# Three norms between GEMM stages by token halves, under neighbouring tiles in half order; value blocks ahead of the projections; squares added on GpSimd

## The reference

```
def rms_norm(x, g):
    xf = x.astype(jnp.float32)
    y = xf * lax.rsqrt(jnp.mean(xf * xf, axis=-1, keepdims=True) + EPS)
    return (y * g.astype(jnp.float32)).astype(x.dtype)
...
        h = modulate(rms_norm(x, g_ffn1[l]), sh1, sc1)
        x = x + HALF_STEP * gt1 * swiglu(h, w_gu1[l], w_down1[l])
        h = modulate(rms_norm(x, g_mix[l]), sh2, sc2)
        x = x + gt2 * hybrid_mixer(h, w_in[l], gate_bias[l], g_q[l], g_k[l], g_mh[l], w_out[l])
        h = modulate(rms_norm(x, g_ffn2[l]), sh3, sc3)
        x = x + HALF_STEP * gt3 * swiglu(h, w_gu2[l], w_down2[l])
        x = rms_norm(x, g_final[l])
```

## Time and profile before

| | us |
|---|---|
| time, median of 3 runs | 3765.18 (3762.93 to 3768.85) |
| the profiled execution's own time | 3765.66 |
| its span | 3763.9 |
| TensorE busy | 3433.6 (91%) |
| VectorE busy | 1844.4 (49%) |
| ScalarE busy | 1248.7 (33%) |
| GpSimd busy | 216.6 (6%) |

### The profile page before, as it was taken

The page is one execution under the profiler, slowest core; times in us unless marked ns, Lnnn a source line. Parts: engine busy times, 40 slices in busy tenths (PEclk is TensorE's granted clock), DMA queues, the critical chain, the costliest instruction groups (busy, mean ns, idle before and its releaser), DMA issues.

```text
span 3763.9 us, 38813 instructions
## 1 busy us (share of the span) xinstructions
PE 3433.6 (91%) x16290; PEld 2754.4 (73%) x16290; DVE 1844.4 (49%) x2135; ACT 1248.7 (33%) x1626; POOL 216.6 (6%) x299
## 2 busy tenths in 40 slices
PE   5999999988897689989999999789889978997996
PEld 3888888866885578868888888458678846776885
DVE  6333333366535679453333333651289556226974
ACT  4111111145231168331111112532168355214753
POOL 0000000000100022000000000010011000101210
PEclk8999999999997699999999999989899989998998
DMA  4222221212742268222212221132342202315221
GB/s 193 99 71 76 93 76 67 79 68 90 178 153 84 54 95 95 69 79 73 90 62 84 84 90 45 35 107 86 109 57 40 76 11 86 114 68 102 45 62 45
DMA packets 156269, 309.73 MB, mean 82 GB/s; under 512 B 55256, under 2 KB 103164, under 8 KB 145088
## 3 DMA queue, kind: packets, MB, share of 16 engines
q1 hardware_dynamic: 95936, 215.52, 17.6%
q0 software_dynamic: 60160, 91.74, 11.2%
HBM read 255.04 MB, written 52.18 MB: 82 GB/s over the span
## 4 chain that ended last, share of the span: by engine, by line
PE 79%; DVE 11%; ACT 6%; issue 2%; DMA 2%; SPq 0%; ACTq 0%; DVEq 0%; POOL 0%
PE psum L612 58%; PE psum L881 5%; PE psum L895 4%; PE psum L871 4%; PE psum L640 2%; PE psum L975 1%; ACT attn_num L1335 1%; DVE h_lo L1532 1%; PE psum L965 1%; PE psum L711 1%; DVE w_lo L1482 1%; ACT attn_th L1326 1%; DMA fo_alt<-in_alternating 1%; PE psum L805 1%; DVE p_u L1619 1%
## 5 line engine op out<-in xcount | busy, mean ns | idle before, releaser
L612 PE MATMUL psum<-h_hi,w_hi 128*128 128x512 f32 x2112 | 833.5, 395 | 45.2 <-DVE h_lo L1532 26.8
L612 PE MATMUL psum<-h_lo,w_hi 128*128 128x512 f32 x2112 | 824.8, 391 | 0.0
L612 PE MATMUL psum<-h_hi,w_lo 128*128 128x512 f32 x2112 | 824.7, 390 | 0.0
L612 PEld LDWEIGHTS psum<-h_hi,w_hi 128*128 128x128 f32 x2112 | 398.3, 189 | 143.5 <-issue 46.3
L612 PEld LDWEIGHTS psum<-h_lo,w_hi 128*128 128x128 f32 x2112 | 398.7, 189 | 83.1 <-issue 2.7
L612 PEld LDWEIGHTS psum<-h_hi,w_lo 128*128 128x128 f32 x2112 | 398.2, 189 | 83.6
L1088 ACT ACTIVATE w_hi<-w_raw 128x2048 fp32r<-128x2048 f32 (+2 forms) x135 | 226.2, 1676 | 538.6 <-PE psum L612 454.8
L1482 DVE TENSOR_TENSOR w_lo<-w_raw,w_hi 128x2048 fp32r<-128x2048 f32 (+2 forms) x135 | 269.4, 1995 | 253.2 <-ACT w_hi L1088 252.5
L1581 DVE TENSOR_TENSOR gate<-gate,psum 128x1024 f32<-128x1024 f32 x44 | 53.7, 1221 | 608.1 <-PE psum L612 608.1
L612 PE MATMUL psum<-a_hi,w_hi 128*128 128x512 f32 x704 | 274.1, 389 | 3.4 <-DVE a_lo L1583 3.4
L612 PE MATMUL psum<-a_lo,w_hi 128*128 128x512 f32 x704 | 273.9, 389 | 0.0
(11 more groups left out here) (356 smaller groups left out, 5111.3 us busy)
## 6 DMA issues: line engine op xcount, KB each, us to landing
w_raw<-in_w_ada SPq DMA_DIRECT2D x52, 1024.0 KB, 4.9
w_raw<-in_w_gu SPq DMA_DIRECT2D x44, 1024.0 KB, 5.3
w_raw<-in_w_in SPq DMA_DIRECT2D x34, 1024.0 KB, 4.9
w_raw<-in_w_down SPq DMA_DIRECT2D x24, 512.0 KB, 3.6
w_raw<-in_w_out SPq DMA_DIRECT2D x12, 1024.0 KB, 6.3
w_raw<-in_w_down SPq DMA_DIRECT2D x16, 640.0 KB, 4.8
qk_hi_scratch<-p_out_hi POOLq DMA_DIRECT2D x18, 512.0 KB, 2.9
qk_lo_scratch<-p_out_lo POOLq DMA_DIRECT2D x18, 512.0 KB, 3.8
```

The lines of the kernel that those rows point to most:

```text
L612: mm = e.matmul(p.half[h], a[:, k * width + m * P:k * width + (m + 1) * P], b(k)[:, h * HALF:(h + 1) * HALF], start=(ends[0] and k == orde ...
```

## The change

It concerns FFN 1, the mixer's projection, the end of the mixer and FFN 2.

- **Half order.** The last down group of an FFN and `out_proj`'s tiles 4 to 7 are done for all tiles on half 0 and then for all tiles on half 1, each tile half in a bank of its own (`take_bank`). The last group has two blocks of 4 x 512 columns in place of four of 4 x 256. `x` is updated by halves; half 0's statistics product comes after the first tile of half 1, and its norm (`guess_half`, `shifted`, `modulated` as generators, stepped between the updates) runs beside the rest of half 1. Half 1's statistics product and norm run in the next stage.
- **Openings.** FFN stages begin with `opening`: the four tiles of gate/up blocks 0 and 1 on half 0, then on half 1; the statistics' pair is the fourth tile's place (`over`). `proj1` begins with the value blocks 4 and 5, half 0 of both and then half 1 of both. In the plan no `ada` block follows gate/up 0 and two follow gate/up 1.
- **GpSimd** adds the squares (`add_squares`) for the tiles in half order, in place of VectorE.
- In `proj1` the gate block follows the k blocks, and the last two ropes run on under blocks 12 and 6; the fence `proj1b` and the row work start behind block 6, not 12. `proj1` stages through two buffers in place of three. `sq` becomes one tensor of 1024 columns, activations `h` are kept by halves, and tiles are placed anew in SBUF so that a norm's tiles and the stage before it don't overlap.

```
-PROJ_ORDER = (0, 1, 2, 3, 4, 5, 12, 6, 7, 8, 9, 10, 11)
+PROJ_ORDER = (4, 5, 0, 1, 2, 3, 12, 6, 7, 8, 9, 10, 11)
+LAST_GROUP = len(FF_GROUPS) - 1
...
+V_ORDER = ((4, 0), (5, 0), (4, 1), (5, 1))
+P1_ORDER = [("v", 2 * (b - 4) + half) for b, half in V_ORDER] + [("qk", i) for i in range(8)]
...
     def plan_ffn(n):
         for kind, i in ffn_order():
             if kind == "gu":
                 plan.append(("w", ins[f"w_gu{n}"][i], (BLK,), ("gu", n, i)))
-                plan_ada(1)
+                plan_ada({0: 0, 1: 2}.get(i, 1))
             else:
-                for c in range(4):
-                    plan.append(("w", columns(ins[f"w_down{n}"][FF_START[i]:FF_START[i + 1]], c), (FF_GROUPS[i], 256),
-                                 ("down", n, i, c)))
+                for c in range(4 if i < LAST_GROUP else 2):
+                    plan.append(("w", columns(ins[f"w_down{n}"][FF_START[i]:FF_START[i + 1]], c, 256 if i < LAST_GROUP else HALF),
...
-        if b >= 4:
+        if b == 3 or b >= 6:
...
+        def opening(stage, stat, tiles_, hi, lo, between):
+
+
+            pp = []
+            for h in range(2):
+                for j, (n_, whi, wlo, key, emptied) in enumerate(tiles_):
+                    if h == 0:
+                        pp.append(ps.take(e, key, *emptied) if j < 3 else ps.over(ps.give(("stat", stat)), key, *emptied))
+                    mm = tile(pp[j].half[h], j % 2, h, KT, whi, wlo, hi, lo,
+                              ready_at=(lambda k, h: h_lo.at(stage, k, h)) if j == 0 else None)
+                    if h == 0 and j == 0:
+                        between()
+                    if h == 1:
+                        mm.then_inc(*tile_done.mark(*key))
+                        if j % 2:
+                            tile_done.value[("block", n_)] = tile_done.count
...
+        def stat_half(stage, h, acc, *event):
+
+            e.wait_ge(*summed_g.at(*event))
+            mm = e.matmul(ps.of[("stat", stage)].half[h], mean1024, acc[:, h * HALF:(h + 1) * HALF], start=True, stop=True)
+            mm.then_inc(*sum_done.mark(stage, h))
...
+            places = [block(("gu", n, i)) for i in range(2)]
+            tiles_ = [(*places[i], (what, n, i), (emptied, n, i))
+                      for i in range(2) for what, emptied in (("gate", gate_silu), ("up", gated))]
+            opening(stage, stat, tiles_, hi, lo, (lambda: None) if n == 1 else
+                    (lambda: stat_half("after mix", 1, t.mix1.acc, "mix", KT - 1, 1)))
...
+                places = [block(("down", n, i, c)) for c in range(2)]
+                ps.take(e, ("stat", after), norm, "var", after, 1)
+                ps.keep(("stat", after))
+                for h in range(2):
+                    for dd in range(KT):
+                        n_, whi, wlo = places[dd // 4]
+                        bank = ps.take_bank(e, ("down", n, i, dd, h), x_new, stage, "half", dd, h)
+                        mm = tile(bank, dd % 4, h, nf, whi, wlo, a_hi_, a_lo_, width=HALF,
+                                  ready_at=(lambda k, h: a_lo.at(n, f0 + k)) if h == 0 and dd == 0 else None)
+                        mm.then_inc(*tile_done.mark("down", n, i, dd, h))
+                        if h == 1 and dd == 0:
+                            stat_half(after, 0, f.g, stage, KT - 1, 0)
...
+            places = {b: block(("in1", b)) for b in (4, 5)}
+            for j, (b, half) in enumerate(V_ORDER):
+                key, (n_, whi, wlo) = ("in1", 2 * b + half), places[b]
+                p = ps.take(e, key, out_lo, key) if j < 3 else ps.over(ps.give(("stat", "after ffn1")), key, out_lo, key)
+                gemm_rows(p, key, half, whi, wlo, m.h, ready_at=(lambda k, h: h_lo.at("mix", k, h)) if b == 4 else None,
+                          between=(lambda: stat_half("after ffn1", 1, t.ffn[1].g, "ffn1", KT - 1, 1)) if j == 0 else None,
+                          block_end=n_ if half else None)
...
+            places = [block(tag + (c,)) for c in (2, 3)]
+            after = f"after {stage}"
+            ps.take(e, ("stat", after), norm, "var", after, 1)
+            ps.keep(("stat", after))
+            for h in range(2):
+                for dd in range(4, KT):
+                    n_, whi, wlo = places[dd // 2 - 2]
+                    bank = ps.take_bank(e, ("out", name, dd, h), x_new, stage, "half", dd, h)
+                    mm = tile(bank, dd % 2, h, KT, whi, wlo, hi, lo, order=order)
+                    mm.then_inc(*tile_done.mark("out", name, dd, h))
+                    if h == 1 and dd == 4:
+                        stat_half(after, 0, m.acc, stage, KT - 1, 0)
...
+            blocks.get(("down", n, LAST_GROUP, 0))
+            e.wait_ge(*a_lo.at(n, FF_TILES - 1))
+            place, m = Counter(), t.proj1
+            front = shifted("mix", m.norm, m.h, 3, 0) if n == 1 else iter(())
+            for h in range(2):
+                for dd in range(KT):
+                    square_half(stage, dd, h, f.g, place)
+                    if h == 1 and n == 1:
+                        if dd == 0:
+                            guess_half("after ffn1", m.norm, 0)
+                        if dd == 3:
+                            blocks.get(("down", n, LAST_GROUP, 1))
+                        if 3 <= dd < 7:
+                            steps(front, 2)
...
+            blocks.get(("down", n, LAST_GROUP, 0))
+            m = t.proj1
+            front = modulated("mix", "after ffn1", m.norm, m.h, "g_mix", 3, 4, 0) if n == 1 else iter(())
+            for h in range(2):
+                for dd in range(KT):
+                    c, key = slice(h * HALF, (h + 1) * HALF), ("down", n, LAST_GROUP, dd, h)
+                    e.wait_ge(*tile_done.at(*key))
+                    e.wait_ge(*x_new.at(stage, LAST_GROUP - 1, dd))
+                    e.scalar_tensor_tensor(out=t.x[:, dd, c], in0=ps.of[key], scalar=cols[:, 8 + dd:9 + dd],
+                                           in1=t.x[:, dd, c], op0=ALU.mult, op1=ALU.add).then_inc(
+                        *x_new.mark(stage, "half", dd, h))
+                    if h == 1 and n == 1:
+                        steps(front, {1: 1, 3: 2, 4: 2, 5: 2, 6: 2, 7: 2}.get(dd, 0))
+                        if dd == 4:
+                            blocks.get(("down", n, LAST_GROUP, 1))
...
+        front = modulated("ffn2", "after mix", f.norm, f.h, "g_ffn2", 6, 7, 0)
+        for h in range(2):
+            for dd in range(4, KT):
+                c, key = slice(h * HALF, (h + 1) * HALF), ("out", "mix1", dd, h)
+                e.wait_ge(*tile_done.at(*key))
+                e.scalar_tensor_tensor(out=t.x[:, dd, c], in0=ps.of[key], scalar=mod_cols(0, 5)[:, dd:dd + 1],
+                                       in1=t.x[:, dd, c], op0=ALU.mult, op1=ALU.add).then_inc(*x_new.mark("mix", "half", dd, h))
+                if h == 1:
+                    steps(front, {4: 0, 5: 4, 6: 5, 7: 3}[dd])
+                    if dd == 5:
+                        blocks.get(("out1", 3))
...
+        def add_squares(stage, items, acc):
+
+            place = Counter()
+            for dd, h in items:
+                c = slice(h * HALF, (h + 1) * HALF)
+                e.wait_ge(*squared.at(stage, dd, h))
+                if dd == 0:
+                    continue
+                j = place.next()
+                if dd == 4 and stage == "mix":
+                    e.wait_ge(*summed.at(stage, 3, h))
+                elif dd == 1:
+                    e.wait_ge(*squared.at(stage, 0, h))
+                else:
+                    e.wait_ge(*summed_g.now())
+                e.tensor_tensor(acc[:, c], acc[:, c], sqh[j % 2], ALU.add).then_inc(*summed_g.mark(stage, dd, h))
+                summed_g.value[(stage, "place", j)] = summed_g.count
```

More of the change, by code:

```diff
@@ L195, in step, with steps @@
             pending.remove(g)
+def steps(generator, n=99):
+    for _ in range(n):
+        next(generator, None)
 class Counter:
@@ L336, in memory @@
         with ExitStack() as sc:
-            f.h = split(f"h{n}", [P, KT, S], sc)
-            f.norm = modulated_tiles(f"nf{n}")
+            back = halves(f"h{n}b", sc)
+            with ExitStack() as over:
+                if n == 1:
+                    gap("norm", 32 * 1024, over)
+                f.norm = modulated_tiles(f"nf{n}", over)
             f.ah = rings(f"a{n}_hi", A_SLOTS, [P, S], F32R, sc)
@@ L341, in memory @@
             f.g = sb(f"gate{n}", [P, S], F32, sc)
+            f.h = list(zip(halves(f"h{n}a", sc), back))
     def rope_tiles(m, name, scope):
@@ L353, in memory @@
     with ExitStack() as hs:
-        m.h = split("hm", [P, KT, S], hs)
-        m.norm = modulated_tiles("nm")
+        front = halves("hma", hs)
         with ExitStack() as sc:
@@ L366, in memory @@
             m.QB = sb("ml_QB", [P, S], F32, sc)
+        with ExitStack() as sc:
+            gap("a_hi", 16 * 1024, sc)
+            m.norm = Box()
+            m.norm.t = rings("nm_t", 4, [P, HALF], F32, sc)
+            gap("a_lo", 16 * 1024, sc)
```

(25 more changed lines are left out.)

396 lines of the change are left out of this document (221 added, 175 removed).

## The result

The changed kernel takes 3826.22 us (median of 4 runs, 3824.84 to 3827.53) against 3767.01 us for the kernel before on the same chip; the ratio is 1.016, 95% interval 1.0148 to 1.0173. The direction was forecast, the size was not: +59 where +24 stood, and outside the range of 3775 to 3803. The profiled execution has a span of 3823.6 us. The page's first row (busy us, share of the span, instructions of each engine) shows TensorE busy 12.8 us longer than before, and in the rest of the 59.7 us by which the span grew, 47 us, it stands.

A forecast was written before the change was run, and what follows sets the result against it. The prediction took TensorE's GEMM as the bound, with 38 us at two norm borders all the edit could give. Terms (a) to (i) summed to +24.4 us, giving 3790 us, range 3775 to 3803.

The forecast's parts named there:

- (a): FFN 1's start: the first product waits for block 1's split instead of a bank, +1.6 us.
- (b): Third gate/up block of each opening: its raw buffer is held by an ada block, stalls of 4.9 and 5.4 us.
- (c): Last down group of both FFNs: TensorE waits for the second block's split, stall 6.8 less 1.7, +5.1 us each.
- (d): out_proj: the fourth block's split, until now hidden by tiles 4 and 5, makes TensorE wait, +6.8 us.
- (g): Norm before FFN 2: stall of 11.2 us, 15.2 us outside GEMM against 19.5, so -4.3 us.
- (i): Behind FFN 2: shorter half updates and squares, GpSimd's longer add, statistics product and wait put inside, +0.7 us.
- (h): Lower TensorE clock after waits: 2.0 us behind each of five new stalls in (b), (c) and (d), +10.0 us.
- (f): proj1: the 5.08 us wait at L640 goes, -5.1 and -1.9 us of clock; the rope turns' waits stay.
- (e): Norm before the mixer: TensorE stands 10.4 us, 14.8 us outside GEMM with clock against 18.7, so -3.9 us.
- rival 3: GpSimd and VectorE slow each other in the norms: upper bound +11 us, so 3801; chance 0.08.
- Rivals 1 and 2: 1: second block's split comes in time, 3752, chance 0.08; 2: only the third block is in time, 3775, chance 0.09.
- rival 1: Second block's split comes in time, so waits of (b), (c), (d) don't show: -13 us, 3752; chance 0.08.

The follow-up runs named there:

- late wait: Changed kernel, but TensorE waits for each list's second weight block only ahead of its first product with it: 3774.29 us, ratio 1.0011.
- four edits: Changed kernel with second-block wait delayed, block behind FFN 2's last group prepared, gate tile's bank emptied first, ada blocks reordered: 3729.79 us, ratio 0.9901.

## Why the size was wrong

**What held.** (a) +1.6, measured +1.4. (b) Stalls of 4.9 (its pieces give 15.7 less 10.9, so 4.8) and 5.4, measured 4.0 and 3.8: the sum of six pieces was 1 to 1.5 us too long. (c) 6.8, measured 6.64 and 6.44; the rows cited for it give 750.7 less 744.1, so 6.6. (d) 6.8, measured 6.73. (g) 11.2, measured 11.01. (i) within the forecast's 4.7 for its stretch, measured 4.6. The late wait shows the cause of six of the stalls in one run: (a), (c) twice, (d), (e) and (g). By these terms alone the forecast of a slower kernel was right for its reason.

**(h), the clock,** was a little small. The granted clock of the changed kernel in windows behind three of the stalls (window, its length, PE busy with products, granted clock, DMA share, GB/s):

```profile
757.52:763.00 5.48, 5.48 (x13) 0.52 0.58 193
763.00:769.00 6.00, 6.00 (x28) 1.00 0.00 1
112.65:118.00 5.35, 5.35 (x13) 0.53 0.60 196
1700.10:1705.00 4.90, 4.90 (x14) 0.65 0.61 214
```

Behind the stall of 6.64 us (first row) thirteen products take 5.48 us at 0.52, half of full speed, where 24 fit at 0.2267 us each: 2.5 us lost, where I took 2.0. After that it is 1.00. Behind the stall of 4.02 us 2.4 us are lost, nearly as much. Behind that of 3.79 us (last row) it is 1.7 us, because the low clock comes only with the sixth product:

```profile
1701.14 0.39 PE L660 MATMUL psum<-h2a_lo,w_hi 128*128 128x512 f32 x1
1701.36 0.55 PE L660 MATMUL psum<-h2a_hi,w_lo 128*128 128x512 f32 x1
1701.71 0.63 PE L660 MATMUL psum<-h2a_hi,w_hi 128*128 128x512 f32 x1
```

Over the five stalls of the term that makes about 11.6 us instead of 10.0. The Trainium skill (TensorE: Matmul & The Clock Gate, HAM oscillation) says that bursts parted by waits start at the lower clock each time. This trace agrees behind the stalls of 4.02 and 6.64 us, and not behind that of 3.79 us, whose burst began at full rate.

**The step that failed first** stands in no term of the sum. It is the sentence "The rest of the kernel is GEMM that the edit does not shorten", with the description's claim that the edit leaves the second layer as it is but for names: the start of the second layer was put at nothing. I priced the instructions at each border, but did not follow who asks for the block after the last one. ScalarE and VectorE prepare a block at a call that the edit moved into an `if` for FFN 1. That left 23.4 us outside the sum, 40% of the result, and the run with that call restored takes 26 back. The range had no room for it, since no rival was about a block that nobody prepares.

**(f), the projection,** failed in one of its pieces. The 5.08 us at L640 are gone, and the 5.16 us at 965.57 too. But "the ada block and split queued there move to the gate tile: 0" was costed by VectorE's time and not by what TensorE takes next: a chunk's transposes take a bank pair behind the gate tile, and ScalarE holds the gate tile's pair for 10.6 us. The forecast had nothing for it. The run with the gate tile first takes the wait away.

**(e), the mixer's norm,** was too cheap by the wait: 13.3 us against 10.4. The extra is less than what the contention costs. Counted from the rows, VectorE lost 1.3 us in two scalings at 794.90 (2.75 for two, where two take 1.4), 1.0 each at 799.55, 806.10 and 810.41, and 0.3 in the Newton step: 4.7 us; other pieces were 2 us quicker than counted. So rival 3's mechanism, to which I gave 0.08 as a case that excludes the forecast, acts in it as well: about half of its upper bound of 11 us. I had taken nothing, since GpSimd's adds on 64 partitions beside VectorE kept their length; but those rows said nothing of what VectorE paid. The Trainium skill (GPSIMD Engine Reference, Specifications) says that the two share their SBUF interfaces and that there is contention with VectorE's instructions that have two SBUF inputs. This trace agrees, with 1.75 us for such an instruction beside an add and 0.74 without. What that cost the kernel is small: with the adds on VectorE the changed kernel took about 5 us less, and the one with four edits the same.

The mixer's row of the table is 13.9 us above its forecast. Of these, 10.6 are the wait for the gate tile's pair and some 2.5 the clock behind it, 2.9 are (e), 0.5 the clock of (c); against them the wait of 5.16 us went, which I had left standing, and the rope turns' waits came out 0.8 us longer (13.5 for six, 12.7 before). That makes 12, and about 2 less if the clock behind the 5.16 us is counted; the other 2 to 4 us I cannot place.

Rivals 1 and 2 are excluded by the waits of 6.4 to 6.7 and 3.8 to 4.0 us. But the late wait shows what rival 1 was right about: the second split is in time when TensorE asks for it only where it first needs it. With that and the other three edits the change gains 37 us. That this is close to the 38 us that the borders held confirms nothing, since some of it comes from waits inside the projection.

## What to carry over

Where an edit lets an engine use two buffers in turn, let it wait for the second when it comes to it, not at the head of the list: here that alone decided between 1.004 and 0.990, with the other three faults mended. When a loop is cut into a new order, follow for each engine who starts the work for the stage after it, and past the last iteration too; here a block that was prepared by a call which the new order no longer makes cost 26 us. And for each new user of a bank count the takes until its pair comes round again, and who empties it by then.

## What the hardware showed

GpSimd and VectorE hold each other up in both directions. Where GpSimd's add was running, a VectorE instruction with two SBUF inputs took 1.75 us instead of 0.74. Where VectorE ran such instructions back to back, GpSimd's add took 7.01 us instead of 1.29, and VectorE kept its 0.75:

```profile
1636.16 7.01 POOL L2349 TENSOR_TENSOR mix_acc<-mix_acc,sq 128x512 f32<-128x512 f32 x1 [7.01 <-ACT sq L1231]
```

```profile
1636.65 0.75 DVE L1699 SCALAR_TENSOR_TENSOR nf_t<-x,cols,nf_r 128x512 f32<-128x512 f32 x1
1637.31 0.75 DVE L1680 SCALAR_TENSOR_TENSOR h2a_lo<-nf_t,mod,h2a_hi 128x512 fp32r<-128x512 f32 x1
```

That add came while a VectorE instruction was running and was held through the eight that followed; it ended 1.2 us after VectorE began, at 1641.95, an update that reads PSUM. The adds at 799.28 and 805.60 also came while a VectorE instruction was running, but took 1.50 and 1.70 us and held up the next one. In the run with the late wait the longest add of the same eight is 7.03 us again, in the run with four edits 1.73. So either side can be the one that waits; what decides it no run here shows. A median duration does not show it either: nm_t had a median of 0.748 us with a longest of 1.782.
